# Pairing the SSM input matmuls on two row groups and two banks, four-part modulation rows, and an earlier first normalisation

## What is computed

```python
mod = silu(c) @ w_ada + b_ada            # one vector of 2048 against 2048 x 12288
sh1, sc1, g1, sh2, sc2, g2 = split(mod, 6)
h = rms_norm(x, norm_mix_g) * (1 + sc1) + sh1
u, q, k, v, ga, gb = split(h @ w_in)     # 2048 x 8192
bu = einsum('blgp,gnp->blgn', u, bbar)   # 64 groups of 16 channels, 64 complex states each
s  = associative_scan(abar, bu)          # along the tokens
y  = gelu(einsum('blgn,gpn->blgp', s, c) + d_skip * u); y_ssm = y * sigmoid(y @ w_glu + b_glu)
merged = sigmoid(ga) * (y_ssm @ w_proj_ssm) + sigmoid(gb) * (attention(q, k, v) @ w_proj_attn)
x = x + g1 * (merged @ w_out)
h2 = rms_norm(x, norm_mlp_g) * (1 + sc2) + sh2
x = x + g2 * (square(relu(h2 @ w_ff1)) @ w_ff2)
# then a second block: recurrent branch, windowed attention, gates, feed-forward, final norm
```

## Time and profile before

| | us |
|---|---|
| median of three runs | 3119.71 |
| runs | 3111.24, 3121.69, 3119.71 |
| the profiled execution's own time | 3117.74 |
| its span | 3116.4 |
| TensorE busy in the span | 3030.4 |
| VectorE busy in the span | 2062.4 |

### The profile page before, as it was taken

How to read it: one execution, slowest core, us unless ns; L and a number is a source line. 1 busy time by engine, 2 the same in 40 slices (tenths; PEclk the granted TensorE clock), 3 DMA queues, 4 the chain that set the end, 5 groups by cost and what they waited for, 6 DMA issues and landing times.

```text
span 3116.4 us, 48463 instructions
## 1 busy us (share of the span) xinstructions
PE 3030.4 (97%) x20187; PEld 2738.1 (88%) x20187; DVE 2062.4 (66%) x2372; ACT 1389.7 (45%) x1700; POOL 243.1 (8%) x253
## 2 busy tenths in 40 slices
PE   6999999899999999999999999999999999999998
PEld 2799989899888888889999999999898888888887
DVE  6778777688676755556787776666556745555555
ACT  3333324433543434444556654544445544444443
POOL 6734320000000000000000000000000000000000
PEclk8999999999999999999999999999999999999999
DMA  8855668788577766564555555446555656566664
GB/s 330 305 183 175 182 212 281 251 301 305 176 255 254 250 203 189 193 189 156 189 155 171 177 183 157 149 150 176 184 192 168 187 187 184 198 186 196 187 192 154
DMA packets 303513, 632.05 MB, mean 203 GB/s; under 512 B 21857, under 2 KB 26353, under 8 KB 302721
## 3 DMA queue, kind: packets, MB, share of 16 engines
q1 hardware_dynamic: 298496, 618.74, 61.2%
q0 software_dynamic: 2000, 4.88, 0.5%
q10 hardware_dynamic: 2800, 5.33, 0.5%
HBM read 624.66 MB, written 4.21 MB: 202 GB/s over the span
## 4 chain that ended last, share of the span: by engine, by line
PE 87%; DVE 6%; DMA 4%; ACT 2%; issue 1%; SPq 0%; ACTq 0%; DVEq 0%
PE PS L1012 19%; PE PS L999 12%; PE PS L1000 11%; PE PS L1001 11%; PE PS L1016 10%; PE PS L1028 7%; PE PS L1030 7%; PE PS L1029 7%; DMA raw<-in_w_in 1%; DVE wlo L1939 1%; DMA F<-in_w_ada 1%; ACT whi L2473 1%; DMA raw<-in_w_ada 1%; PE PS L774 1%; DVE aacc L1928 1%
## 5 line engine op out<-in xcount | busy, mean ns | idle before, releaser
L1939 DVE TENSOR_TENSOR wlo<-raw,whi 128x1024 fp32r<-128x1024 f32 x867 | 1084.3, 1256 | 787.9 <-ACT whi L2473 786.5
L2473 ACT ACTIVATE whi<-raw 128x1024 fp32r<-128x1024 f32 x867 | 914.3, 1059 | 1161.1 <-PE PS L1001 431.8
L999 PE MATMUL PS<-R,whi 128*128 128x256 f32 x3584 | 1033.3, 288 | 24.9 <-DVE wlo L1939 17.4
L1000 PE MATMUL PS<-R,whi 128*128 128x256 f32 x3584 | 1020.0, 285 | 0.0
L1001 PE MATMUL PS<-R,wlo 128*128 128x256 f32 x3584 | 1019.6, 284 | 0.0
L999 PEld LDWEIGHTS PS<-R,whi 128*128 128x128 f32 x3584 | 693.8, 194 | 46.9 <-DVE wlo L1939 24.9
L1000 PEld LDWEIGHTS PS<-R,whi 128*128 128x128 f32 x3584 | 694.1, 194 | 0.6 <-issue 0.5
L1001 PEld LDWEIGHTS PS<-R,wlo 128*128 128x128 f32 x3584 | 693.7, 194 | 0.0
L1012 PE MATMUL PS<-R,whi 128*128 128x512 f32 x2496 | 628.5, 394 | 10.8 <-DVE R L1849 5.4
L1012 PEld LDWEIGHTS PS<-R,whi 128*128 128x128 f32 x2496 | 451.8, 190 | 92.7 <-issue 11.5
L1016 PEld LDWEIGHTS PS<-R,wlo 128*128 128x128 f32 x2496 | 342.2, 191 | 24.6
(11 more groups left out here) (415 smaller groups left out, 1870.7 us busy)
## 6 DMA issues: line engine op xcount, KB each, us to landing
raw<-in_w_in SPq DMA_DIRECT2D x283, 512.0 KB, 4.2
raw<-in_w_ff SPq DMA_DIRECT2D x176, 512.0 KB, 4.2
raw<-in_w_ada SPq DMA_DIRECT2D x144, 512.0 KB, 5.2
raw<-in_w_mlp_up SPq DMA_DIRECT2D x128, 512.0 KB, 4.1
raw<-in_w_mlp_down SPq DMA_DIRECT2D x128, 512.0 KB, 4.2
F<-in_w_ff SPq DMA_DIRECT2D x80, 512.0 KB, 4.4
raw<-in_w_out SPq DMA_DIRECT2D x53, 512.0 KB, 4.4
F<-in_w_ada SPq DMA_DIRECT2D x48, 512.0 KB, 6.4
```

The source lines that it names most:

```text
L999: pe.matmul(o, whi[:, s, c:c + P], x.operand.hi(k), start=first, stop=False, skip_group_check=True)
L1000: pe.matmul(o, whi[:, s, c:c + P], x.operand.lo(k), start=False, stop=False, skip_group_check=True)
L1939: v.tensor_tensor(wlo[:, i % SPN, :], words(j), whi[:, i % SPN, :].bitcast(F32), ALU.subtract).then_inc(lo_done, 1)
L2473: a.activation(whi[:, i % SPN, :], words(j), ACT.Copy).then_inc(hi_done, 1)
```

## The change

Four things are altered.

1. **SSM inputs.** The two calls of `inputs` for a pass, one ahead of the output part and one behind it, become one loop behind it. It alternates the two row groups e = 0, 1 with each matrix, and group e writes bank 4 + e. So a pass now takes both banks 4 and 5, and its matmuls wait for `scan_done` of the pass just before (until now: of the pass before that). `bu_done` counts once a pass. VectorE's rotation and its scans each move one tick forward.
2. **Rows.** `row_matmuls` multiplies four pieces of 256 columns into partitions 0, 32, 64 and 96, where it multiplied two of 512 into partitions 0 and 32. `row_copy` takes four copies of 256 where it took two of 512.
3. **First normalisation.** The closing of the first half, its modulation and `norm1` stand at tick -33, where they stood at -32 and -31, and `row_copy` comes ahead of the rounding of weights in its tick.
4. **Weight units in the opening.** `TAKEN` is 33, 35, ..., 63 where it was 37, 38, 40, ..., 63; units 0 and 1 are both prepared in tick -33.

```diff
--- before.py
+++ after.py
@@ -29,8 +29,8 @@
 
 
 NEARLY = 19
-TAKEN = {37 + n * 26 // 15: n for n in range(16)}
-EARLY = {a - 3: (n,) for a, n in TAKEN.items()} | {61 + n: (16 + n,) for n in range(3)}
+TAKEN = {33 + 2 * n: n for n in range(16)}
+EARLY = {31: (0, 1)} | {a - 3: (n,) for a, n in TAKEN.items() if n > 1} | {61 + n: (16 + n,) for n in range(3)}
 NWIDE = 56
 NXN = 16
 SSM0 = 23
@@ -271,7 +271,7 @@
     ct2 = [x.rearrange("p (f s) -> p f s", f=8) for x in ct2_]
     xh_ = [RF[:, 10240:11264], RF[:, 11264:12288], *ct2_]
     half_sum = lambda i: RF[:, 8192 + 1024 * i:9216 + 1024 * i] if i < 2 else RF[:, 10240 + 1024 * i:11264 + 1024 * i]
-    pairs_bu = lambda i: PS[:, 4 + i % 2, :].rearrange("p (e c n) -> p e c n", e=2, c=2)
+    pairs_bu = PS[:, 4:6, 0:T].rearrange("p e (c n) -> p e c n", c=2)
     ebase = (GB, E0)
 
     def etable(ft):
@@ -520,7 +520,7 @@
 
     acc_tick = {units[j][1]: n for n in TICKS for j in prepared(n) if units[j][0] == "acc"}
 
-    close_tick = [-32, len(TAKEN)] + [n for n, bank in closes]
+    close_tick = [-33, len(TAKEN)] + [n for n, bank in closes]
     assert all(acc_tick[16 * g + 15] < close_tick[g] for g in range(2, 10))
 
     close_bank = [4, 4] + [bank for n, bank in closes]
@@ -590,7 +590,7 @@
 
     X_TURN, COLUMNS, X_SUMS = -NADA + 6, -NADA + 10, -NADA + 12
     B_TURN, MATRICES, MATRICES_C = -NADA + 24, -NADA + 40, len(TAKEN) + 4
-    ROW_CLOSE, NORM1 = [-32, len(TAKEN)], [-31, len(TAKEN) + 1]
+    ROW_CLOSE, NORM1 = [-33, len(TAKEN)], [-33, len(TAKEN) + 1]
 
 
 
@@ -674,9 +674,9 @@
                 pe.wait_ge(*v_once.at("cact"))
             if q and kt == 0:
                 wait_bank(row_bank[1])
-            for half in range(2):
-                o = 32 * half
-                t = pe.matmul(PS[o:o + 1, row_bank[q], :], cact[:, kt:kt + 1], words(j)[:, half * 512:half * 512 + 512],
+            for part in range(4):
+                o = 32 * part
+                t = pe.matmul(PS[o:o + 1, row_bank[q], 0:T], cact[:, kt:kt + 1], words(j)[:, part * T:part * T + T],
                               start=(kt == 0), stop=(kt == 15))
             t.then_inc(row_done, 1)
 
@@ -766,22 +766,7 @@
 
             pe.wait_ge(m_copied, 8)
 
-            def inputs(i, e):
-                ft, j, bank = i // 2, i % 2 * 2 + e, 4 + i % 2
-                rs = slice(32 * j, 32 * j + 32)
-                for ci in range(2):
-                    o = PS[:, bank, (2 * e + ci) * HALF:(2 * e + ci + 1) * HALF]
-                    pe.matmul(o, lb2[rs, ci, ft, :], u_even[rs, ft, :], start=True, stop=False, skip_group_check=True)
-                    t = pe.matmul(o, lb[rs, ci, ft, :], u_odd[rs, ft, :], start=False, stop=True, skip_group_check=True)
-                t.then_inc(bu_done, 1)
-
             for i in range(18):
-                if i < 16:
-                    if i % 8 == 0:
-                        pe.wait_ge(evac_v["u"], i // 8 + 1)
-                    wait_bank(4 + i % 2)
-                    inputs(i, 0)
-                    free[4 + i % 2] = (scan_done, i + 1)
                 r = i - 2
                 if r >= 0:
                     ft, j0 = r // 2, r % 2 * 2
@@ -806,12 +791,21 @@
                                           start=(ci == 0), stop=(ci == 1), skip_group_check=True)
                     t.then_inc(y_done, 1)
                     free[yb] = (yg_ready, ft + 1)
-                else:
-                    yield from ssm_pause(4 * i)
                 if i < 16:
-                    pe.wait_ge(bu_done, 2 * i + 1)
-                    inputs(i, 1)
-                for p in range(int(r < 0), 4):
+                    ft, j0 = i // 2, i % 2 * 2
+                    if i % 8 == 0:
+                        pe.wait_ge(evac_v["u"], i // 8 + 1)
+                    wait_bank(4)
+                    wait_bank(5)
+                    for ci in range(2):
+                        for m, u_ in ((lb2, u_even), (lb, u_odd)):
+                            for e in range(2):
+                                rs = slice(32 * (j0 + e), 32 * (j0 + e) + 32)
+                                t = pe.matmul(PS[:, 4 + e, ci * HALF:ci * HALF + HALF], m[rs, ci, ft, :], u_[rs, ft, :],
+                                              start=(m is lb2), stop=(m is lb), skip_group_check=True)
+                    t.then_inc(bu_done, 1)
+                    free[4] = free[5] = (scan_done, i + 1)
+                for p in range(4):
                     yield from ssm_pause(4 * i + p)
 
         def bias_tiles():
@@ -1330,7 +1324,8 @@
             two = lambda a: a.rearrange("p (h c) -> p h c", h=2)
             b = row_close_bank[g] if kind == "row" else close_bank[g]
             sums = PS[:, b:b + 2, 0:4] if kind == "row" else two(PS[:, b, 0:8])
-            yield
+            if g:
+                yield
             v.wait_ge(*((row_turned, g + 1) if kind == "row" else (acc_turned, g + 1)))
             v.tensor_tensor(two(mod[:, o:o + 8]), sums, two(cols[:, C_BADA + o:C_BADA + o + 8]),
                             ALU.add).then_inc(modrow if kind == "row" else modacc, 1)
@@ -1341,19 +1336,18 @@
                 ft, j0 = i // 2, i % 2 * 2
                 Ec, Es = etable(ft)
                 cc, sn = Ec[:, j0:j0 + 2, :], Es[:, j0:j0 + 2, :]
-                z, bu = zz_[i % 2], pairs_bu(i)
-                for p in range(2):
-                    yield from ssm_pause(4 * i + p)
+                z, bu = zz_[i % 2], pairs_bu
+                yield from ssm_pause(4 * i)
                 if j0 == 0:
                     v.wait_ge(*e_at(ft))
-                v.wait_ge(bu_done, 2 * i + 2)
+                v.wait_ge(bu_done, i + 1)
                 if i > 1:
                     v.wait_ge(z_used, i - 1)
                 v.tensor_tensor(z[:, :, 0, :], bu[:, :, 1, :], sn, ALU.mult)
                 v.tensor_tensor(z[:, :, 1, :], bu[:, :, 0, :], sn, ALU.mult).then_inc(rot_done, 1)
                 v.wait_ge(rot_done, 2 * i + 1)
                 v.tensor_tensor(bu, bu, cc.unsqueeze(2).broadcast_to([P, 2, 2, HALF]), ALU.mult).then_inc(rot_done, 1)
-                yield from ssm_pause(4 * i + 2)
+                yield from ssm_pause(4 * i + 1)
                 v.wait_ge(rot_done, 2 * i + 2)
                 v.tensor_tensor(bu[:, :, 0, :], bu[:, :, 0, :], z[:, :, 0, :], ALU.add).then_inc(v_own, 1)
                 first = vt.one()
@@ -1365,7 +1359,8 @@
                         k = 2 * i + e
                         t = v.tensor_tensor_scan(z[:, e, c, :], mag2[:, k:k + 1].broadcast_to([P, HALF]), bu[:, e, c, :], 0.0, ALU.mult, ALU.add)
                 t.then_inc(scan_done, 1)
-                yield from ssm_pause(4 * i + 3)
+                for p in (2, 3):
+                    yield from ssm_pause(4 * i + p)
 
         def gelu(ft):
             yb = 6 + ft % 2
@@ -2108,8 +2103,9 @@
             a.wait_ge(row_done, 16 * q + 16)
             if q:
                 a.wait_ge(row_turned, q)
-            for o in (0, 32):
-                t = a.copy(aacc[o:o + 1, 0:512], PS[o:o + 1, row_bank[q], :])
+            for part in range(4):
+                o = part // 2 * 32
+                t = a.copy(aacc[o:o + 1, part % 2 * T:part % 2 * T + T], PS[32 * part:32 * part + 1, row_bank[q], 0:T])
             t.then_inc(row_copied, 1)
 
         def matrices():
@@ -2464,6 +2460,8 @@
         def main(n):
             if n == -NADA:
                 setup()
+            if n in (-33, -1):
+                row_copy(0 if n == -33 else 1)
             for j in prepared(n):
                 if units[j][0] == "w":
                     i = units[j][1]
@@ -2494,8 +2492,6 @@
                 new.append(matrices())
             if n == MATRICES_C + 1:
                 new.append(matrices_c())
-            if n in (-33, -1):
-                row_copy(0 if n == -33 else 1)
             if n in NORM1:
                 new.append(norm1(NORM1.index(n)))
             new += [gelu(ft) for ft in range(8) if n == phase_tick(13 + 8 * ft)]
```

## The result

The changed kernel takes 3096.39 us (median of 6 runs, 3095.67 to 3101.34). The kernel before takes 3115.43 (6 runs, 3111.24 to 3121.69). The ratio is 0.9943, with a 95% interval of 0.9932 to 0.9953. So it is faster by 0.6%, and 2.6 us under the forecast. The profiled execution took 3096.35 us, 21.4 less than that of before.

What follows compares the result with a forecast made beforehand. TensorE bounds the SSM stretch and from 600 us on; VectorE, then fetches, the opening. Gains 17.9 - 1.5 + 1.8 + 0.3 + 1.5 = 20.0 us gave 3099.7 against the median, stated as 3099 us, range 3090 to 3112.

Steps and rivals of the forecast that it cites:

- The sum of the passes: SSM passes: input matmuls 1.08 us instead of 2.20, 17.9 us gained over 16 passes, less 1.5 us of waiting.
- The stall: SSM passes 1 and 2: TensorE waits for VectorE's scans of the pass before, taken as 1.5 us lost.
- The slack: SSM pass 3: scans end at 241.2 us, TensorE asks for them at 245.8, so 4.6 us to spare.
- no overlap: Rival, SSM inputs: row groups run one by one, 2.04 us a pass; passes give 2.6 us, time 3113 to 3114; chance 0.09.
- The opening: Stretch up to pass 0: rows, first normalisation and 110 to 146 us together gain 3.6 us.
- pass 0 not before 182 us: Sign of being wrong: first SSM pass starts no sooner than 182 us; 3 to 4 us sooner than 182.38 was forecast.
- The row groups on the chain, +1.8: Opening: three row multiplications on the path take half as long, 2.0 us less, of which 1.8 is taken.
- The first normalisation, +1.5: Opening: two splits fill VectorE's idle time ahead of the first modulation; 1.5 us gained, ends 0 and 2.5.
- If the second split ends 1 us after the modulation could have run: Opening, first normalisation: if the rounded units come too late for VectorE's splits, `norm1` is that much later.
- 110 to 146 us, +0.3: Opening, where fetches set the pace: shorter rows beside waits for tiles gain 0.3 us.
- The rival of the opening: Opening gives nothing: lower clock from less dense TensorE, or splits too late; time 3103 to 3106; chance 0.17.
- The other signs: Opening: first weight unit before 71 us, pass 0 3 to 4 us sooner, VectorE's wait before first modulation below 1 us.

Runs made afterwards that it cites:

- SSM edits alone: Kernel before with only the new SSM part (alternating inputs, rotation and scans one tick forward), old rows, normalisation and weight units: 3098.11 us, ratio 0.9948.
- opening edits alone: Kernel before with only four-part rows, first normalisation at tick -33 and the new weight units, old SSM inputs: 3115.49 us, ratio 1.0005.
- the kernel with the old rows: Changed kernel with two row matmuls of 512 columns and two copies again, all else as changed: 3099.71 us, ratio 0.9955 to the kernel before.

## Why the prediction was right

**The sum of the passes held.** It was 17.9 - 1.5. A pass fell by 1.10 where 1.12 was forecast, from a row of another kernel part with 64-row groups. Eight matmuls took 1.11 us, where 1.08 was worked out. The 0.055 us for each row holds for 32-row groups as well. The entry cost of 0.2 us is contained in it. The terms as forecast give 16.4, and 16 x (2.20 - 1.11) - 1.4 gives 16.0. Between the SSM edits alone and the opening edits alone, which lost the same to the clock, the stretches differ by 16.3 us. The two profiles of the result differ by 19.2, of which 3.4 are the lower clock at pass 0 of the kernel before: 15.8 without it. The clock is also what spreads that stretch. It took 232.0 and 233.4 us with the old passes and 214.2 to 218.7 with the new ones from tick 23 (alternating, and with the scans where the change puts them), and with the time lost to the clock taken out 230.0 to 230.3 and 213.6 to 214.2.

**The stall came out by luck.** 1.5 us were taken for the wait for the scans in passes 1 and 2. That wait was 0.4 us. The other 1.0 is the output part of pass 2 (L783), which waits for the output matrices that VectorE makes at L1291. No term of mine had that wait. It is new because TensorE now reaches that place sooner.

**The slack was there.** On VectorE, the scans of pass 3:

```profile
233.90 1.34 DVE L1360 TENSOR_TENSOR_SCAN F<-pw,PS 128x128 f32<-128x128 f32 x4
```

They end at 235.24, and TensorE asks at 240.88: 5.6 us, where 4.6 was forecast. One tick later costs 2 us of waits and two ticks cost 6, which brackets it.

**What "no overlap" is worth wasn't tested.** My 2.04 us for it fits the 2.0 us that the spacing of the records gives. But placing group after group isn't that case, since the groups overlap at the change-over, by 0.34 us. So half of the gain of a pass doesn't need the alternation, which I hadn't seen. The Trainium skill (TensorEngine Tiling (Array Packing), Key Properties) has a change of tiling mode drain TensorE. One change fewer a pass explains at most the 0.2 us of the entry.

**The opening was mis-sized: 3.6 us forecast, none that can be told from 0 measured.** Pass 0 is at 182.39, 184.43 and 183.44 with the changed opening (181.0 to 185.03 in six executions with that opening, 183.1 in the mean), and at 182.38 and 183.61 with the old one. I had named "pass 0 not before 182 us" as a sign of being wrong, and for the opening it was right. Its terms, one by one:

- *The row groups on the chain, +1.8.* The 2.06 us are there at 37.71. At 57.89, where the last sum starts, 1.5 us of them are left. So this term was right in its place and lost behind it.
- *The first normalisation, +1.5.* This is the step that failed. I let the two splits fill VectorE's idle time ahead of the modulation. But they wait for ScalarE, which first takes `row_copy` (1.49 us for the four copies against 1.16) and then 2.00 us for the roundings. So VectorE idles 2.51 us and splits behind that, for 2.78 us, ahead of the modulation. I had named this case, "If the second split ends 1 us after the modulation could have run", and taken the middle. The way from `row_copy` to the modulation is so 1.4 us longer, which takes back what the rows had brought. The clock did the same at the same moment: L705 took 3.58 us at the lower clock. Either alone would have done it: the kernel with the old rows shows the splits with the closing at full clock (5.0 us), the SSM edits alone show the lower clock with the old order (5.3 us).
- *110 to 146 us, +0.3.* The granted clock fell to 0.93 from 0.99 and the DMA share stayed at 0.95, where it was 0.98. Nothing is seen to be gained in a stretch that the fetches set. By 75 us all executions had fetched 25.1 to 25.2 MB, whatever stood in the opening before.

**The rival of the opening** named both causes, the clock and splits that come too late, and no gain of the opening is what came. Its price was too high: I had added up to 7 us of slow weight units to the missing gain. That the whole still came within 3 us of the forecast is in part luck. In the two profiled executions the missing 3.6 us are made up by the 3.4 us that the kernel before lost to the clock at pass 0, and by 2.2 us behind the passes.

**The clock of the timed runs** bears that rival out further than the profiles do. With two-part rows the mean granted clock is 0.9873, 0.9876 and 0.9868 for the kernel before (21, 14 and 9 runs), 0.9876 for the SSM edits alone (5) and 0.9876 for the old rows (5). With four-part rows, passes from tick 23 and no extra matmuls it is 0.9852 to 0.9859 in all seven kernels (51 runs). The old rows differ from the changed kernel in the rows alone, so the short rows go with 0.0019 less. The opening edits alone have 0.9854, 0.0019 less than before, which is 6 us of TensorE's work at full clock, an estimate and an upper one: where TensorE waits, a lower clock costs nothing. That is more than the 3.6 us that are missing. So it may be that the opening does save what I summed and that the clock takes it back. Which of the lost clock falls on the path isn't shown.

At the first closing the rows show this much. With the four-part rows and nothing added, L705 took 3.57 to 3.58 us in all nine executions. With two-part rows it took 1.95 in two and 3.57 in one.

**The other signs.** The first weight unit starts at 67.06, before 71 as forecast. Pass 0 isn't 3 to 4 us sooner. VectorE's wait ahead of the modulation isn't below 1 us.

## What to carry to other kernels

Small matmuls that use a few rows of TensorE gain in two ways when they are placed as one block over several row groups and banks: here 0.54 us for the one block (0.2 an entry less, 0.34 an overlap where one group follows the other) and 0.56 us more for alternating, of 2.2 us in a pass. A shorter step on the path is worth what it frees at the next point where two chains meet; before filling an engine's idle time with other work, add up the whole way of that work (here copies, roundings, splits: 5.3 us) and compare it with the way that it delays (3.9 us). When a bank is shared between passes, the distance in ticks between its last reader and its next writer is the thing to count: with 5.6 us of slack, one tick of 2.9 us later cost 2 us of waits and two ticks 6. And before a difference of a few us is put down to an edit, the mean granted clock of the runs should be compared: here 0.001 of it is 3 us.

## What the runs showed of the hardware

- The 16 records of eight float32 matmuls of 128 columns on 32-row groups take 1.11 us when two groups and two banks alternate, 1.67 us when one group follows the other in two banks, and 2 x 1.10 us as two calls in one bank each. In the second case the groups overlap by three rows at the change-over.
- The same 16 closing matmuls with one column (L705) take 1.95 or 3.58 us, and identical code ahead of them gave both: 1.95 in the kernel before, 3.57 with its opening and the new passes.
- Row multiplications of half the length went with a lower mean granted clock over the whole kernel: 0.9852 to 0.9859 in 51 runs with four parts of 256 columns, 0.9868 to 0.9876 in 54 runs with two of 512.
- Extra matmuls that keep the clock up cost more than it gives: six, some 8 us in all, turned a 3.58 us closing into one of 1.95 us and moved its start from 59.49 or 60.25 to 64.30.
